# A one-layer streaming encoder step: rows of the front's end loaded earlier, the values product transposed, index scores moved, the token table in two parts

## The reference

```python
sh1, sc1, gt1, sh2, sc2, gt2 = split(silu(c) @ w_mod + b_mod, 6)
h = rms_norm(x, g_mix) * (1 + sc1) + sh1
qa, ka, va, qi, ki, wi, qg, kg, vg, lr, rg = split(h @ w_in)
# group A: an index score picks the keys, 8 query heads over 2 key/value heads attend to them
iscore = einsum('bqh,bqhl->bql', wi, relu(einsum('bqhd,bld->bqhl', qi, ki)))
sel = top_k(masked(iscore), k)                      # 128 keys (prompt), 256 (sample)
oa = softmax(qa @ ka[sel].T / 8) @ va[sel]
# group B: gated linear attention in chunks, per-head norm, gated by silu(rg)
ob = rms_norm(gla(qg, kg, vg, log_sigmoid(lr @ w_gate + b_gate) / 16), g_out) * silu(rg)
x = x + gt1 * (concat(oa, ob) @ w_out)
h = rms_norm(x, g_ffn) * (1 + sc2) + sh2
x = x + gt2 * experts(h)                            # top 4 of 32, clamped SwiGLU of width 1024
y = rms_norm(x, g_final) * (1 + scale) + shift      # scale, shift from c and w_mod_final
```

## Time and profile before

| | us |
|---|---|
| three timed runs | 1576.58, 1580.65, 1581.11; median 1580.65 |
| the profiled execution | 1578.06, of it the span that the profile covers 1576.4 |
| experts' first product | 466.39 |
| TensorE busy in the span | 1447.4 (92%) |
| VectorE, ScalarE, GpSimd busy | 714.4, 196.5, 291.1 |

### The profile page before, as it was taken

One profiled execution on the slowest core, in us unless ns is written; L12 is line 12 of the kernel. 1 busy time (PEld: TensorE's weight loads), 2 busy tenths in 40 slices (PEclk: granted clock), 3 DMA queues, 4 the chain that ended last, 5 costly groups with the idle time before them and its releaser, 6 DMA issues.

```text
span 1576.4 us, 38017 instructions
## 1 busy us (share of the span) xinstructions
PE 1447.4 (92%) x15948; PEld 677.9 (43%) x15948; DVE 714.4 (45%) x1672; ACT 196.5 (12%) x461; POOL 291.1 (18%) x412
## 2 busy tenths in 40 slices
PE   4997999998949999999999999999999999999854
PEld 3755647773523344334334433343333433343311
DVE  1787793445543353344334433443334433443327
ACT  2312434451100000000000000000000000000101
POOL 0362032210011112111211121112111121112040
PEclk8998999999869999999999999999999999999957
DMA  9941118926478999999999999999999999996983
GB/s 338 260 151 54 54 54 309 342 69 249 181 293 341 416 422 420 419 418 420 420 419 418 421 419 419 419 420 421 418 419 419 421 419 419 418 420 267 406 279 121
DMA packets 89568, 528.69 MB, mean 335 GB/s; under 512 B 21178, under 2 KB 26604, under 8 KB 64172
## 3 DMA queue, kind: packets, MB, share of 16 engines
q1 hardware_dynamic: 59784, 468.18, 72.7%
q0 software_dynamic: 27088, 52.70, 10.2%
q10 hardware_dynamic: 2644, 7.10, 1.3%
HBM read 499.91 MB, written 27.88 MB: 335 GB/s over the span
## 4 chain that ended last, share of the span: by engine, by line
PE 66%; DMA 25%; DVE 5%; issue 2%; ACT 1%; POOL 1%; SPq 0%; DVEq 0%; POOLq 0%; ACTq 0%
PE psum L1825 24%; DMA down_w<-in_w_down 22%; PE psum L1832 20%; PE psum L1631 7%; PE psum L1791 3%; PE psum L1639 2%; PE psum L1610 2%; DMA front_ring<-in_w_mod 2%; PE psum L1880 1%; PE psum L1768 1%; PE psum L1801 1%; DMA work<-in_w_router 1%; PE psum L1814 1%; PE psum L1583 1%; PE psum L1738 1%
## 5 line engine op out<-in xcount | busy, mean ns | idle before, releaser
L1832 PE MATMUL psum<-down_w,expert_work 128*32 128x256 f32 x6208 | 348.2, 382 | 22.9 <-DMA down_w<-in_w_down 22.3
L1825 PE MATMUL psum<-gu_even,expert_work 128*32 128x512 f32 x3136 | 342.4, 596 | 9.9 <-DVE expert_work L1294 8.9
L1825 PE MATMUL psum<-gu_odd,expert_work 128*32 128x512 f32 x3072 | 332.6, 592 | 0.0
L1299 DVE TENSOR_TENSOR expert_work<-psum,expert_work 128x512 f32<-128x512 f32 x97 | 64.3, 663 | 503.9 <-PE psum L1825 503.9
L1832 PEld LDWEIGHTS psum<-down_w,expert_work 128*32 128x32 f32 x6208 | 201.1, 110 | 183.7 <-issue 32.3
L1546 POOL DMA_DIRECT2D ys_dram<-expert_work x97 | 70.0, 722 | 822.6 <-DVE expert_work L1314 787.9
L1825 PEld LDWEIGHTS psum<-gu_even,expert_work 128*32 128x32 f32 x3136 | 103.1, 110 | 238.8 <-issue 234.5
L1825 PEld LDWEIGHTS psum<-gu_odd,expert_work 128*32 128x32 f32 x3072 | 101.5, 110 | 221.3 <-issue 218.6
L837 ACT ACTIVATE expert_work<-expert_work 128x256 f32<-128x256 f32 x97 | 40.4, 417 | 979.3 <-DVE expert_work L1301 979.3
L1631 PE MATMUL psum<-front_ring,work 128*128 128x512 f32 (+2 forms) x320 | 115.3, 520 | 0.0
L1540 POOL DMA_INDIRECT expert_work<-h_dram,keep x100 | 99.0, 990 | 48.9 <-POOL keep L1536 26.9
(11 more groups left out here) (345 smaller groups left out, 1091.8 us busy)
## 6 DMA issues: line engine op xcount, KB each, us to landing
gu_even<-in_w_gate_up SPq DMA_DIRECT2D x68, 2048.0 KB, 21.8
down_w<-in_w_down SPq DMA_DIRECT2D x66, 2048.0 KB, 18.9
gu_odd<-in_w_gate_up SPq DMA_DIRECT2D x64, 2048.0 KB, 22.8
front_ring<-in_w_mod SPq DMA_DIRECT2D x12, 2048.0 KB, 8.9
ys_dram<-expert_work POOLq DMA_DIRECT2D x97, 128.0 KB, 14.8
front_ring<-in_w_in SPq DMA_DIRECT2D x4, 2048.0 KB, 11.1
front_ring<-in_w_mod_final SPq DMA_DIRECT2D x4, 2048.0 KB, 9.9
front_ring<-in_w_out SPq DMA_DIRECT2D x2, 2048.0 KB, 10.4
```

The lines of the kernel that those rows point to most:

```text
L1299: v.tensor_tensor(gu_s[g_], psum[:, g_, :], bias_b[:, 0:2 * QW], ALU.add).then_inc(gu_added, 1)
L1825: last = mm(psum[GT * u:GT * u + GT, g_, :], lhsT=xT[:, g_, k, :], rhs=w[:, :, u * QW:(u + 1) * QW], start=(k == 0), stop=(k == KD - 1))
L1832: last = mm(down_sum(g_)[GT * u:GT * u + GT, :], lhsT=actT[g_][:, k, :], rhs=dn_slot(c)[:, k % 4, u * QW:(u + 1) * QW], start=(k == 0), st ...
```

## The change

- **Order of the steps.** The index scores of tiles 1 to 3 stand between the four gate projections instead of ahead of them; the transposes of the queries follow.
- **Values product.** VectorE makes, for each unit, a diagonal matrix of the reciprocal row sums for each of the two heads (`make_diag`), at its `sc` step two units later (for the last two units at `pT`). `pT` becomes a product of the probabilities with this diagonal, and `pv` multiplies with the values as the stationary operand, so that its result comes out transposed: two key/value heads on two halves of the partitions, in turn. VectorE only copies it, into `cat_t`. `catT` is left with group B's four blocks; the rows of `w_out` are loaded in the order of the heads, in three loads a chunk instead of one.
- **Rows.** GpSimd issues the rows of the end at its step `("pT", 3, 0)` instead of at `catT`; the tiles are laid out anew, so that they lie beside what the attention still uses. What VectorE does with the rows moves ahead, to `catT`.
- **Table.** VectorE works out row and group first as if there were no overflow, makes the one-hots of groups 0 to 95, then the overflow's groups and theirs. TensorE makes the table in two parts (`table`, `table2`); the gathers of the first expert wait for the first part only. The clearing of `brow` moves ahead.
- **Weights of the first experts.** Chunk 3 of expert 0 is loaded after the last modulation chunk, the others after the last `y`. The second expert's gate/up, which now lies over tiles of the table, is loaded after `over`.

```diff
-    s += [("idx", t, h) for t in range(1, SAMPLE) for h in range(NIH)]
+    for j in range(4):
+        s += [("idx", j + 1, h) for h in range(NIH) if j + 1 < SAMPLE]
+        s.append(("qkg", j))
     s += [("qaT", t) for t in ORDER] + [("ckT",)]
-    s += [("qkg", j) for j in range(4)]
...
-    s += [("rank",), ("table",), ("over",)]
+    s += [("rank",), ("table",), ("table2",), ("over",)]
...
+                if c[0] == "out":
+                    cols = slice(c[1] * CW, (c[1] + 1) * CW)
+                    for g_ in range(2):
+                        sp.dma_start(wslot(s)[HD * g_:HD * g_ + HD, 0:4, :], w_heads[g_, :, :, cols]).then_inc(loaded[s], 16)
+                    sp.dma_start(wslot(s)[:, 4:KD, :], w_out[:, 4:KD, cols]).then_inc(loaded[s], 16)
+                    continue
...
+            filled(sp, JOB[("mod", MODS - 1)])
+            load_gu(0, 3, 0)
             for t in range(T):
-                filled(sp, JOB[("catT", t)])
-            sp.wait_ge(rows_in, ROW_DMAS * 16)
+                filled(sp, JOB[("y", t)])
             for c in range(3):
                 load_gu(0, c, 0)
-            for t in range(T):
-                filled(sp, JOB[("y", t)])
-            load_gu(0, 3, 0)
             for c in range(DNC):
                 load_dn(c, 0)
-            filled(sp, JOB[("hT", ORDER[-1])])
+            sp.wait_ge(brow_clear, 1)
+            bias_rows(0)
+            in_sbuf(sp, ("over",))
...
             for c in range(GUC):
                 load_gu(1, c, 1)
-            sp.wait_ge(brow_clear, 1)
-            bias_rows(0)
...
+            def make_diag(u):
+                two = 1 if UNITS[u][0] == SAMPLE else 2
+                dve.wait_ge(probs_made, u + 1)
+                if u >= 2:
+                    filled(dve, JOB[("pT", *UNITS[u - 2])])
...
+                r1 = rinv[:, 2 * (u % 4):2 * (u % 4) + two]
+                order(v.reciprocal(r1, ars[:, 2 * (u % 4):2 * (u % 4) + two]))
+                for x in range(two):
+                    ins = v.tensor_scalar(diag[u % 2][:, x, :], ident, r1[:, x:x + 1], None, ALU.mult)
+                ins.then_inc(diag_ready, 1)
...
+                elif kind == "pT" and UNIT[s[1:]] >= len(UNITS) - 2:
+                    make_diag(UNIT[s[1:]])
...
+                    if kind == "sc" and u >= 2:
+                        make_diag(u - 2)
                     filled(dve, j)
...
-                    if t != SAMPLE:
-                        r2_ = rinv[:, 2 * (u % 4):2 * (u % 4) + 2]
-                        order(v.reciprocal(r2_, ars[:, 2 * (u % 4):2 * (u % 4) + 2]))
-                        v.tensor_tensor(catA[0:R, t, :].rearrange("p (g r d) -> p g r d", g=2, r=PAIRS)[:, :, h, :],
-                                        bank(j)[0:R, 0:2 * HD].rearrange("p (g d) -> p g d", g=2),
-                                        r2_[0:R].unsqueeze(2).to_broadcast([R, 2, HD]), ALU.mult).then_inc(done, 1)
+                    else:
+                        v.tensor_copy(cat_t[:, h, tok], bank(j)[:, 0:P]).then_inc(done, 1)
                         gla_norm(s)
...
+                    def hot_groups(lo_, hi_):
+                        for i in range(T):
+                            cols = slice(TOPE * i, TOPE * (i + 1))
+                            v.tensor_tensor(at_group[:, cols, lo_:hi_], iota_g[:, lo_:hi_].unsqueeze(1).to_broadcast([P, TOPE, hi_ - lo_]),
+                                            f6[:, cols].unsqueeze(2).to_broadcast([P, TOPE, hi_ - lo_]),
+                                            ALU.is_equal).then_inc(hot_made, 1)
+
+                    hot_groups(0, GB * NE)
...
+                    hot_groups(GB * NE, NG)
+                elif kind == "table":
+                    filled(dve, j)
+                    v.tensor_scalar(tab[:, 0:GB * NE], bank(j)[:, 0:GB * NE], quart, None, ALU.add).then_inc(done, 1)
+                    v.memset(brow, 0.0).then_inc(brow_clear, 1)
...
+                elif s == ("pT", 3, 0):
+                    in_sbuf(pool, ("go", SAMPLE))
+                    in_sbuf(pool, ("pv", SAMPLE, 1))
+                    pool.wait_ge(out_state, 32)
...
-                    pe.wait_ge(probs_made, u + 1)
+                    pe.wait_ge(diag_ready, u + 1)
...
-                            last = tr(group(j)[:, x * P:(x + 1) * P], prob[u % 3][:, at_:at_ + P], ident)
+                            last = mm(group(j)[:, x * P:(x + 1) * P], lhsT=prob[u % 3][:, at_:at_ + P],
+                                      rhs=diag[u % 2][:, x // nb, :], start=True, stop=True)
...
-                        for g_ in range(2):
-                            for x in range(nb):
-                                last = mm(bank(j)[:, HD * g_:HD * g_ + HD],
-                                          lhsT=pT[u % 2][:, (g_ * nb + x) * P:(g_ * nb + x + 1) * P],
-                                          rhs=va[:, x, HD * g_:HD * g_ + HD], start=(x == 0), stop=(x == nb - 1))
...
+                        for x in range(nb):
+                            for g_ in range(2):
+                                half = slice(HD * g_, HD * g_ + HD)
+                                last = mm(bank(j)[half, 0:P], lhsT=va[:, x, half],
+                                          rhs=pT[u % 2][:, (g_ * nb + x) * P:(g_ * nb + x + 1) * P],
+                                          start=(x == 0), stop=(x == nb - 1))
...
-                    for k in range(KD):
-                        src = catA[0:R, t, k * P:(k + 1) * P] if k < 4 else rg[0:R, t, (k - 4) * P:(k - 3) * P]
-                        last = tr(group(j)[:, k * R:(k + 1) * R], src, ident[0:R, 0:R])
+                    for k in range(4):
+                        last = tr(bank(j)[:, k * R:(k + 1) * R], rg[0:R, t, k * P:(k + 1) * P], ident[0:R, 0:R])
```

More of the change, by code:

```diff
@@ L311, in build @@
         qaTs = csg
-        osum = [cc[:, 0:64], cc[:, 64:128]]
+        cat_t = catA_flat[:, 0:4 * NTOK].rearrange("p (k n) -> p k n", k=4)
+        diag = [qgT[:, 0, n * 2 * P:(n + 1) * 2 * P].rearrange("p (g n) -> p g n", g=2) for n in range(2)]
         pT = [at.take(1024), qi_flat]
@@ L315, in build @@
         ars = at.take(16)
-        op = Carver(work_t, WORK)
-        catT = op.take(KD * NTOK).rearrange("p (k n) -> p k n", k=KD)
-        rowP = [op.take(D) for _ in range(3)]
-        rowS = [op.take(D) for _ in range(3)]
-        gffn_b = op.take(D)
-        xin = [op.take(D), op.take(D)]
+        early = Carver(work_t, WORK)
+        early.take(STAGE_AT)
+        rowP = [early.take(D) for _ in range(3)]
+        rowS = [early.take(D) for _ in range(3)]
+        gffn_b = early.take(D)
+        wr = early.take(KD * NE).rearrange("p (k n) -> p k n", k=KD)
+        br_b = early.take(NE)
+        early.take(26400 - early.at)
+        v8 = early.take(T * 8)
+        e4 = early.take(T * TOPE)
+        gs1 = early.take(T)
+        op = Carver(work_t, GUC * SLOT)
+        gated_t = op.take(4 * NTOK).rearrange("p (k n) -> p k n", k=4)
         x2b = [op.take(D), op.take(D)]
@@ L484, in build @@
                 last_step[("out", 0)] = last_step[("out", 1)] = s
-        parts = [2 if c[0] == "kv" else 1 for c in chunks]
+        parts = [{"kv": 2, "out": 3}.get(c[0], 1) for c in chunks]
         need = []
@@ L1155, in dve_step @@
                     h = s[2]
-                    u = UNIT[s[1:]]
                     filled(dve, j)
-                    dve.wait_ge(probs_made, u + 1)
-                    if t != SAMPLE:
-                        r2_ = rinv[:, 2 * (u % 4):2 * (u % 4) + 2]
-                        order(v.reciprocal(r2_, ars[:, 2 * (u % 4):2 * (u % 4) + 2]))
-                        v.tensor_tensor(catA[0:R, t, :].rearrange("p (g r d) -> p g r d", g=2, r=PAIRS)[:, :, h, :],
-                                        bank(j)[0:R, 0:2 * HD].rearrange("p (g d) -> p g d", g=2),
-                                        r2_[0:R].unsqueeze(2).to_broadcast([R, 2, HD]), ALU.mult).then_inc(done, 1)
-                        gla_norm(s)
-                        return
-                    r1 = rinv[:, 2 * (u % 4):2 * (u % 4) + 1]
-                    order(v.reciprocal(r1, ars[:, 2 * (u % 4):2 * (u % 4) + 1]))
-                    if t == SAMPLE:
-                        order(v.tensor_scalar(osum[h], bank(j)[:, h * HD:(h + 1) * HD], r1, None, ALU.mult))
-                        for q in range(4):
-                            ins = v.tensor_copy(catA[0:R, t, (4 * h + q) * HD:(4 * h + q + 1) * HD],
-                                                osum[h][32 * q:32 * q + R, :])
-                        ins.then_inc(done, 1)
+                    if t == SAMPLE:
+                        half = slice(HD * h, HD * h + HD)
+                        v.tensor_copy(cat_t[half, :, tok], bank(j)[half, 0:P].rearrange("p (r n) -> p r n", r=PAIRS)).then_inc(done, 1)
+                    else:
+                        v.tensor_copy(cat_t[:, h, tok], bank(j)[:, 0:P]).then_inc(done, 1)
+                        gla_norm(s)
+                elif kind == "catT" and t == ORDER[0]:
```

(19 more changed lines are left out.)

115 lines of the change are left out of this document (57 added, 58 removed).

## The result

The changed kernel takes 1586.78 us, the median of eight runs (1583.32 to 1587.42); the kernel before took 1580.72 beside it (eight runs, 1576.58 to 1584.55). The ratio is 1.0039, 95% interval 1.0028 to 1.0050: slower by 6 us, where 1576.5 and a range of 1567 to 1583.5 were predicted. The profiled execution took 1584.82, its span 1583.2 (before: 1578.06 and 1576.4).

What follows compares the result with a forecast made beforehand. The weight stream sets the time from the expert stage on. The front's +3.3 + 4.3 + 4.0 - 11.3 = +0.3, with the second expert's weights requested earlier, gave -2.7 us: 1576.5 us, range 1567 to 1583.5.

Steps and rivals of the forecast that it cites:

- the line: Weight stream at 0.395 MB/us, drawn back to 20.97 MB: met at 479.7 before, predicted at 477.0; the end follows one to one.
- Part 1: Index scores between gate projections: VectorE's hole of 5.5 us delays kd, idle TensorE then meets slow clock; +3.3 us.
- the rival in which TensorE keeps the gates' gain: Gate projections: VectorE closes its hole, the reordered scores cost 0; -6.0 us, 1573, chance 0.07.
- Part 2, steps 2 to 11: Attention with transposed values product: blocks and values net +1.8, waits for diagonals 2.5; +4.3 us.
- the rival of four transposes: Attention's probability blocks: each product costs four transposes, 0.49 instead of 0.247; +24 us, 1600, chance 0.02.
- Part 2, steps 12 to 15: Attention's steps 12 to 15 with the transposed values product: a gain of 0.3 us by the same prices.
- Part 2, last five steps: Attention's end: the gated norm lies between VectorE's copy and the next diagonal; 21.6 us instead of 17.3.
- Part 3: Rows loaded amid the attention: VectorE's wait at the first y goes, with TensorE's idle time and slow clock; -11.3 us.
- Part 4: Token table in two parts: gathers start 5.5 us earlier, overflow list read by 455.4 instead of 457.80.
- the rival of the gathers: First expert's gathers drown in the weight stream, 17.7 us each; +9 us, 1587, decided by a start after 468; chance 0.08.
- The attention pays nothing: Attention: VectorE keeps ahead of the diagonals, so the +8 of the values product goes; -10.7 us, 1568.5, chance 0.28.
- Dear diagonals: Attention's diagonals on VectorE: scalings take 0.571 us instead of 0.2; +7 us, 1583.5, chance 0.08.

Runs made afterwards that it cites:

- odd_halves: Changed kernel, two of the second expert's four gate/up chunks requested when the last h2 is stored, the others after the overflow list: ratio 1.0025 to the kernel before.
- scores_ahead: Changed kernel with the index scores of tiles 1 to 3 ahead of all four gate projections again: ratio 1.0002 to the kernel before.
- diag_scores_odd: Changed kernel with diagonals one step earlier, index scores ahead of the gate projections, second expert's gate/up in two halves with the gathers between: 1563.38 us.
- gathers_first: Changed kernel with the second expert's gate/up requested only when the first gathers have landed: ratio 1.0031 to the kernel before.
- table_alone: Kernel before with the token table in two parts and gathers behind the first, second expert's request left at the last h2: ratio 0.9985.

## Why the prediction was wrong, point by point

The mechanisms were the ones named; the sizes were off, the worst of them in one direction, and with them another limit came to count. The forecast put the line at 477.0 by the request of the second expert's weights, at 455.7 + 0.3. They were requested at 461.7, but odd_halves shows that this did not count: the line lies 13.3 us behind TensorE's start, at 486.3. Of those 9.3 us, 6.4 are the front (+6.7 instead of +0.3), the rest the gathers.

| term | predicted | measured |
|---|---|---|
| scores between gates | +3.3 | +5.0: `kd` 1.0, clock 4.0 |
| steps 2 to 11 | +4.3 | +4.3: `kd` to sc(12) 78.77 in scores_ahead, 74.45 before |
| steps 12 to 15 | -0.3 | +0.8 |
| last five steps | +4.3 | +8.8 |
| rows, end of the front | -11.3 | -11.5 to the end of the second y (34.35 for 45.89), -0.8 behind it |
| table to the gathers | -5.5 | -5.2 (rank to GpSimd's copy 15.40 for 20.64) |
| third gather | +2.8 in a start near 464 | +5.2 |

- **Part 1** failed in the clock. VectorE's hole was right (tile 2's scores at 133.29, 132.5 predicted), and so was the idle TensorE; most of the idle time lay at the PSUM bank, and only 2.88 us ahead of `kd`. The 2.0 us of slow clock, taken from one y, were 4.0 here. With `kd` 1.0 later, the rival in which TensorE keeps the gates' gain falls.
- **Part 2, steps 2 to 11** came as costed. diag_scores_odd parts it: `kd` to sc(12) takes 75.93 with early diagonals, so 1.5 are blocks and values (1.8 predicted), 2.8 the diagonals' wait (2.5). The block product is the plain product that the earlier trace rows priced, 2.02 to 2.05 for sixteen records; the rival of four transposes falls. The Trainium skill (TensorE: Matmul & The Clock Gate, Terms) calls the transpose mode four times faster for FP32; in this case's traces it is twice as fast, 1.04 us for 2.02 to 2.05.
- **Part 2, steps 12 to 15** lost 0.8 where 0.3 was to be gained: 0.7 of it is the diagonals' wait, which was not charged there (12.96 us with early diagonals in diag_scores_odd, 12.88 before).
- **Part 2, last five steps** is the step that failed most. From the end of one values product to the end of the next, 4.9 us were predicted for steps 17 and 18, and they took 5.17 each. Step 16 took 7.76 instead of 5.8, steps 19 and 20 8.02 instead of 6.0; in all 26.1 for 21.6. Half clock in two block products, 1.6 each, makes 3.2 of the 4.5 us; I had charged TensorE's waits in part 1 with a price in clock and these with none. The other 1.3 are spread, 0.3 to 0.5 on each of 16, 17, 18 and the last two together.
- **Part 3** was right: no wait ahead of the first `hT`, rows loaded in the attention.
- **Part 4** was right up to the gathers' issue. I had the third gather suffer "some 5 us" and wrote a start near 464 all the same, which leaves it 2.8 (last issue 456.6 and 4.6 on from there, as from 461.82 to 466.39 before). It started at 473, past the 468 from which the rival of the gathers decides, and by that rival's line, 13.3 us after the start, the end follows. This rival, at 0.08, has the time that came, 1587, by luck: it took it from gathers of 17.7 us each. Here they cost 5.2, and the front's 6.4 carried the start past 468.
- **"The attention pays nothing"**, the rival at 0.28, falls for this order of VectorE's work, with 11.8 us of waits. For another order it is right: with early diagonals, in diag_scores_odd, it is 104.7 us from `kd` to the attention's end, before 104.6.
- **"Dear diagonals"** falls: two scalings take 0.48 us (L987 above), 0.24 each and not 0.571.

What stays open: what the gathers' packets wait for in the first 4 us, why a wait of 2.1 us is followed by half clock once and not the other time, and the 1.3 us of the last five steps that the clock does not explain.

## What to carry to other kernels

In a queue that runs in order, what another engine stands for goes ahead of the queue's own wait: the diagonals cost 12 us of attention behind a copy and a norm, and next to nothing a step earlier. A wait on TensorE is priced with the clock behind it, each time, not only where it is long. Small transfers that start a stage come back sooner when they are issued into an empty queue (2.7 us for 5.0 to 8.1); but when the large load goes behind them, as in gathers_first, its late request can take the gain back. With two limits on a stream, moving one brings only what lies between them.

## What the runs showed of the hardware that was not expected

**Gathers behind weights.** In gathers_first, with SyncE's queue empty, all 48 packets of the first gather move from 1.5 to 3 us after its issue at 461.65 (463.1 to 464.6):

```profile
q0 software_dynamic: 48, 0.13, 28.8%
q1 hardware_dynamic: 8, 0.00, 4.4%
```

With weights under way no packet of a gather moves for 4 us in table_alone (above), and in diag_scores_odd from 441.1, where the first gather is issued, to 445.1 there is SyncE's queue and none of GpSimd's:

```profile
q1 hardware_dynamic: 110, 1.77, 104.0%
```

So a first gather meets 2.5 us of delay (4.0 for 1.5) and then half the turns: the third one lands 2.72 to 2.74 us after its issue with an empty queue, 5.0 to 8.1 with weights under way. The Trainium skill (DMA: Bandwidth & Descriptors, Queues, rings and completion order) has each DMA engine take turns between the rings that have work, a packet at a time. The trace agrees from the moment the packets begin, 85 to 87 in table_alone; in the 4 us ahead of it, with 119 packets to none, it shows no turns.

**The clock after short waits.** In the changed kernel TensorE stood 2.12 us ahead of the block product at 350.05, which ran at full clock, 2.02, and 2.13 us ahead of the one at 355.22, which ran at half, 3.59. So in this kernel a wait of 2 us cost nothing or 1.6 us more; behind 2.88 us at `kd` it was 4.0.
